# Strassen products in the output stage of a hybrid delta-rule / HGRN2 block

## What is computed

```python
# ya, yb: gated outputs of the two head groups, 512 channels each
y_lat = jnp.concatenate([ya, yb], axis=-1) @ w_out          # 1024 x 1024
x_lat = x_lat + m_lat[2] * y_lat
h_lat = modulate(rms_norm(x_lat, norm2_g), m_lat[3], m_lat[4])
x_lat = x_lat + m_lat[5] * (jnp.square(jax.nn.relu(h_lat @ w_mlp1)) @ w_mlp2)   # 1024 x 4096, 4096 x 1024
return rms_norm(x_lat, final_g)
```

## Time and profile before

| | |
|---|---|
| runs, us | 3981.03, 3980.72, 3990.34 (median 3981.03) |
| span of the profiled execution, first to last instruction | 3976.3 us |
| PE busy | 3551.1 us (89%) |
| DVE busy | 1828.9 us (46%) |
| ACT busy | 1525.4 us (38%) |
| POOL busy | 891.9 us (22%) |
| front stage | 0 to 108 us |
| merge stage | 2282 to 2364 us |
| output stage | 2364 to 3976 us |

### The profile page before, as it was taken

How to read it: one execution, slowest core, us unless ns; L and a number is a source line. 1 busy time by engine, 2 the same in 40 slices (tenths; PEclk the granted TensorE clock), 3 DMA queues, 4 the chain that set the end, 5 groups by cost and what they waited for, 6 DMA issues and landing times. The chain is left out here.

```text
span 3976.3 us, 98790 instructions
## 1 busy us (share of the span) xinstructions
PE 3551.1 (89%) x42320; PEld 2944.9 (74%) x42320; DVE 1828.9 (46%) x2710; ACT 1525.4 (38%) x2048; POOL 891.9 (22%) x872
## 2 busy tenths in 40 slices
PE   6899999999788888857776649999999999999999
PEld 3677888888677777747666238888888888888887
DVE  5488401110055555536555746444544464445443
ACT  5566314332155555513334313333322342234223
POOL 0220233231145545506555102000100100010001
PEclk8899999999899999966778669999999999999999
DMA  6243433452323333333342573434333333333332
GB/s 252 73 81 64 90 109 134 136 138 74 100 90 109 111 103 107 107 100 87 93 99 59 202 243 96 122 96 120 113 117 99 98 112 117 100 96 112 97 99 85
DMA packets 599112, 441.14 MB, mean 111 GB/s; under 512 B 119949, under 2 KB 548305, under 8 KB 591577
## 3 DMA queue, kind: packets, MB, share of 16 engines
q1 hardware_dynamic: 574048, 408.20, 35.3%
q0 software_dynamic: 5632, 16.78, 1.4%
q10 hardware_dynamic: 19192, 12.65, 1.1%
HBM read 338.17 MB, written 99.39 MB: 110 GB/s over the span
## 5 line engine op out<-in xcount | busy, mean ns | idle before, releaser
L618 PE MATMUL p_pg<-h_hi,p_whi 128*128 128x512 f32 (+1 forms) x1384 | 532.1, 384 | 10.0 <-DVE p_wlo L847 10.0
L2639 ACT ACTIVATE o_w_hi<-o_raw 128x1024 fp32r<-128x1024 f32 x288 | 303.6, 1054 | 573.1 <-PE o_pg L2600 558.7
L618 PE MATMUL p_pg<-h_hi,p_wlo 128*128 128x512 f32 (+1 forms) x1384 | 520.2, 376 | 0.0
L618 PE MATMUL p_pg<-h_lo,p_whi 128*128 128x512 f32 (+1 forms) x1384 | 520.1, 376 | 0.0
L2598 PE MATMUL o_pg<-o_f_hi,o_w_hi 128*128 128x512 f32 x1088 | 425.0, 391 | 0.0
L2600 PE MATMUL o_pg<-o_f_hi,o_w_lo 128*128 128x512 f32 x1088 | 423.6, 389 | 0.0
L2599 PE MATMUL o_pg<-o_f_lo,o_w_hi 128*128 128x512 f32 x1088 | 423.5, 389 | 0.0
L2598 PE MATMUL o_pg<-o_h_hi,o_w_hi 128*128 128x512 f32 x1024 | 400.2, 391 | 1.7 <-DVE o_w_lo L2718 1.7
L2600 PE MATMUL o_pg<-o_h_hi,o_w_lo 128*128 128x512 f32 x1024 | 398.7, 389 | 0.0
L2599 PE MATMUL o_pg<-o_h_lo,o_w_hi 128*128 128x512 f32 x1024 | 398.6, 389 | 0.0
L2718 DVE TENSOR_TENSOR o_w_lo<-o_raw,o_w_hi 128x1024 fp32r<-128x1024 f32 x288 | 351.6, 1221 | 58.3 <-ACT o_w_hi L2639 58.3
(11 more groups left out here) (310 smaller groups left out, 6808.0 us busy)
## 6 DMA issues: line engine op xcount, KB each, us to landing
o_raw<-in_w_mlp SPq DMA_DIRECT2D x256, 512.0 KB, 4.1
g_kqvb<-scr_kqv SPq DMA_DIRECT2D x72, 384.0 KB, 3.4
p_raw<-in_w_in SPq DMA_DIRECT2D x38, 512.0 KB, 6.0
g_kqa<-scr_kqv SPq DMA_DIRECT2D x72, 256.0 KB, 3.0
p_mw<-in_w_mod POOLq DMA_DIRECT2D x64, 256.0 KB, 3.3
o_raw<-in_w_out SPq DMA_DIRECT2D x32, 512.0 KB, 4.2
scr_kqv<-p_y SPq DMA_DIRECT2D x24, 576.0 KB, 5.9
scr_hf<-p_y SPq DMA_DIRECT2D x16, 576.0 KB, 5.5
```

The source lines that it names most:

```text
L618: last = nc.tensor.matmul(pg[0:m, bank, 0:n], w[:, q, k, 0:m], h[bank][:, k, :], start=(k == 0 and j == 0), stop=(k == KT - 1 and j == 2))
L2639: nc.scalar.activation(w_hi[:, i % 2], raw[:, i % 2], ACT.Copy).then_inc(w_hi_ready, 1)
```

## The change

The three products of the output stage are computed as 2 x 2 block products by the Winograd form of Strassen's scheme: each operand is cut in four quadrants, seven products of combined quadrants take the place of eight, and the four result quadrants are put together from them.

*Units.* There are 72 units. Each is a 2 x 2 block product with a stationary operand `s` (256 wide: two halves m of 128), a moving operand `t` (1024 wide: two halves n of 512) and a contraction of 1024 (two halves of four pieces of 128). Each unit has seven steps q = 0 to 6, one per product, of 12 matmuls of 128x512 each (hi·hi, hi·lo, lo·hi for four pieces). Units 0 to 7 (M1 = 8) are w_out: s is 256 tokens of y, t the whole weight. Units 8 to 39 are w_mlp1: s is 256 hidden channels of the weight, t the h of 1024 tokens, in two sets of 16 units. Units 40 to 71 are w_mlp2: s is 256 tokens of f, t a quarter of the weight, four sets of 8 units. "x units" are those of w_out and w_mlp2, "f units" those of w_mlp1.

*Operands.* The seven combinations of s are made per unit by POOL (four subtractions or additions of 128x512: `mix_start`, `mix_turn`, `mix_end`) and split per step by ACT (`s_high`) and DVE (`s_low`), one unit ahead. The seven combinations of t (7 x 128x2048) are held for a whole set. At the last unit of a set SP loads the next seven, 1 MB each, one after each step (`t_load`), ACT rounds them (`t_high`, 128x2048), DVE makes five lo parts and POOL two (`t_low`). There are six such **set changes**, at units 7, 23, 39, 47, 55, 63. The combinations of w_mlp2 are made by POOL during the f units (`pre_join`) and kept in device memory (`scr_w2`), those of h by DVE (`join_operands`), kept in `scr_h`; the ones of w_out are made in the merge stage, with the gate of the residual folded in.

*Results.* Products accumulate in four PSUM banks X, Y, V, Z. Step 0 is read out by ACT (`take_p1`), DVE adds banks and partial sums (`combine` at steps 1 to 6). In x units POOL adds three quadrants to x (`x_add`). In f units ACT applies relu and square. x now stands token-major; x1, h and f go through device memory between the units (`scr_x1`, `scr_h`, `scr_f`). In w_out units ACT also squares, scales and reads back the transposed rows (PE `turn`, 16 transposes of 128x128 per unit, after step 4 of the next unit), to make h.

*Elsewhere.* The front stage no longer stores the transposed x (8 stores of 1 MB on SP); semaphores there are allocated in another way. The final norm is applied by DVE to token-major rows; the transposes at the end are gone.

```diff
 def phase_merge(nc, e):
...
+                w_load(0)
+                w_load(1)
+                sp.wait_ge(rows_ready, 1)
+                sp.dma_start(e.sgate[:, :], mrow[:, :]).then_inc(rows_out, 16)
...
+            @block.gpsimd
+            def _(pool):
+                pool.wait_ge(gate_in, 16)
+                done = 0
+                for kk in range(4):
+                    pool.wait_ge(wo_in[kk % 2], 32 * (kk // 2 + 1))
+                    gate = e.o_gate[:, :].rearrange("p (n c) -> p n c", n=2).unsqueeze(2).to_broadcast([P, 2, 2, TB])
+                    nc.gpsimd.tensor_tensor(lo32[:, 0::2, kk, :].rearrange("p (n h) c -> p n h c", n=2),
+                                            wr[:, kk % 2].rearrange("p (n h) c -> p n h c", n=2), gate, ALU.mult).then_inc(wo_gated, 1)
+                    pool.wait_ge(wo_gated, kk + 1)
+                    done = join_operands(pool, lambda q: lo32[:, q, kk, :], wo_joined, done)
...
+                    if b < NB - 1:
+                        act.wait_ge(wo_joined, 4 * b + 4)
+                        nc.scalar.activation(t_hi[:, :, b, :], lo32[:, :, b, :], ACT.Copy).then_inc(wo_hi, 1)
...
 def phase_out(nc, e):
...
+        BANK = (BX, BY, BX, BY, BV, BZ, BV)
...
+        SETS = [0, M1, M1 + N1 // 2] + [M2 + NW * c for c in range(FC)]
+        LAST_OF = {at - 1: k for k, at in enumerate(SETS) if k}
...
+                def t_load(s, q):
+                    sp.wait_ge(product, 7 * (SETS[s] - 1) + q + 1)
...
+                    sp.dma_start(lo32[:, q], src).then_inc(t_in[q], 16)
...
+                        if q == 0:
+                            if i + 2 < N:
+                                raw_load(i + 2)
+                            if 0 <= i - 2 < M1:
+                                h_store(i - 2)
+                            if pre_step(i - 2) is not None:
+                                pre_store(pre_step(i - 2))
+                        if q == 1 and 0 <= i - 1 < N and not final_unit(i - 1):
+                            store(i - 1)
...
+                def multiply(i, q):
+                    pe.wait_ge(s_lo_ready, 7 * i + q + 1)
...
+                    if q == 1:
+                        pe.wait_ge(u3_ready, i)
+                    if q == 2:
+                        pe.wait_ge(p1_ready, i + 1)
+                    if q == 3:
+                        pe.wait_ge(u2_ready, i + 1)
+                    if q == 4:
+                        pe.wait_ge(c12_ready, i)
+                    if q == 5:
+                        pe.wait_ge(c21_ready, i)
+                    if q == 6:
+                        pe.wait_ge(c22_ready, i + 1)
...
+                    for k in range(4):
+                        nc.tensor.matmul(out, s_hi[:, q, k, :], t_hi[:, q, k, :], start=(not more and k == 0), stop=False,
+                                         skip_group_check=more)
+                        nc.tensor.matmul(out, s_hi[:, q, k, :], t_lo[:, q, k, :], start=False, stop=False, skip_group_check=more)
+                        last = nc.tensor.matmul(out, s_lo[:, q, k, :], t_hi[:, q, k, :], start=False, stop=(k == 3),
+                                                skip_group_check=more)
...
+                def scale(i):
+                    act.wait_ge(inv, i + 1)
+                    act.wait_ge(x1_out[i % 2], 16 * (i // 2 + 1))
...
+                        if i + 1 < N:
+                            s_high(i + 1, q)
+                        if i in LAST_OF and q >= 2:
+                            t_high(LAST_OF[i], q - 2)
+                        if i - 1 in LAST_OF and q < 2:
+                            t_high(LAST_OF[i - 1], q + 5)
...
+                        if 0 <= i < N and q:
+                            combine(i, q)
+                        if i + 1 < N:
+                            s_low(i + 1, q)
+                        if i in LAST_OF and q >= 2:
+                            t_low(LAST_OF[i], q - 2)
```

More of the change, by code:

```diff
@@ L2501, in y_of @@
[L2501 to L2510 removed]
+        raw, t_hi, t_lo, gate = e.o_raw, e.o_t_hi, e.o_t_lo, e.o_gate
+        lo32 = e.o_t_raw
+        s_hi, s_lo = sb("s_hi", [P, 7, 4, P], F32R), sb("s_lo", [P, 7, 4, P], F32R)
```

800 lines of the change are left out of this document (453 added, 347 removed).

## The result

| | before | after |
|---|---|---|
| median of 9 runs each, us | 3980.72 (3974.34 to 3990.34) | 3995.45 (3991.71 to 4007.86) |
| profiled span | 3976.3 | 3991.5 |
| PE, DVE, ACT, POOL busy | 3551.1, 1828.9, 1525.4, 891.9 | 3386.4, 2038.0, 1645.9, 1707.9 |
| first product to last product | 2367.52 to 3957.54, 1590.0 | 2398.59 to 3979.16, 1580.6 |

The account below looks back on a forecast made before the run. TensorE's matmuls were taken to bound the output stage; -196 + 19 + 96 + 27 + 33 - 6 = -27 us gave a span of 3949 and a median of 3954 us, 4.7 above the span, range 3890 to 4035.

Parts of the forecast that it names:

- set changes: Six changes of t in the output stage: late loads, rounding and splitting cost 3 x 11 + 3 x 21 = 96 us.
- w_out units: Units 2 to 6: PE waits 5.4 us each before the transposes for x's store behind h's, 27 us in all.
- Products: Output stage: 6048 matmuls instead of 6912 at the old pace of 0.2269 us, 196 us less.
- f units: w_mlp1 units: a lo part waiting for POOL makes ACT's copy 0.6 us late, 31 times, 19 us.
- The chain: f units, steps 4 to 6: DVE combination, ACT relu, square and hi part, DVE lo part, 3.45 us against PE's 2.72.
- Merge stage and filling: Stage ahead of the output stage and its first operands: w_out loads and POOL's work delay the first matmul, +33 us.
- tail: From the last product to the kernel's end: 12.5 us instead of 18.4, so -6 us.
- front: First stage: dropping the x stores could give at most 1.4 us, counted as 0.
- second rival: f units, steps 4 to 6: every lo part waits for POOL at the shared port, 80 us, 4034 us; chance 0.19.
- clock rival: Output stage: after some 11 long waits 12 matmuls run at half speed, 30 us, 3984, no change; chance 0.09.
- port rule: DVE operations with two SBUF inputs and POOL's SBUF reads exclude each other; without it the sum some 35 us lower.
- 3857: Rival that the output stage's waits are mostly covered: terms sum to -124 us, 3895 its likelier form; chance 0.21.

Follow-up runs that it names:

- e4_no_mix: Changed kernel without POOL's four combinations of s, ACT and DVE taking plain quarters instead: 3996.95 us, ratio to before 1.0047.
- e1_x_first: Changed kernel with SP issuing the store of x ahead of the store of h in w_out units: 3957.02 us, ratio to before 0.9946.
- e5_no_w2: Changed kernel without the w_mlp2 work beside the f units (loads, POOL's long product, 1.75 MB stores): 3981.41 us, ratio to before 1.0.
- e10_four: Changed kernel with x stored before h, t split three steps behind its load, merge split one block later, all t low parts on DVE: 3910.61 us.

## Why the prediction was wrong, point by point

The steps that failed are two terms of the sum, the set changes (96 us forecast, 136 measured) and the w_out units (27 forecast, 53 measured). What they had at nothing or too small was DVE's work ahead of a combination that PE needs, with small operations held for 3.6 to 4.4 us by POOL's long ones, and the slow clock behind the waits. These 66 us less the 17.5 that the f units gave back, and some 6 of small terms, took the forecast of -27 to +15.

- **Products**: right, -197 for -196; the pace held.
- **f units**: over-sized, 1.5 for 19. The chain was sized well: ACT's copy of product 0 ends 9.5 and 10.5 us after product 4, unit by unit in turn, for 10.3, and PE has slack in the first and loses 0.09 us in the second. I let one lo part to a unit wait for POOL at steps 5 and 6; the trace shows DVE's means up (1032 and 1141 ns for 0.69), but in places with slack. e4_no_mix shows what it costs when the long operation comes into the narrow place.
- **w_out units**: the wait named, for x's store behind h's, was right in place, and e1_x_first shows it. Its size, 5.8 for 5.4, is partly luck: the forecast had both stores issued at 6 us and only the bytes of h as the hindrance, where SP stood for DVE's additions until 9 us, and PE came to the place 2.5 us later too. What the step left out made it 53 instead of 27: the combination behind DVE's four additions (2.0 a unit), and the fallen clock in the transposes and behind them (about 2.6). The clock stood among the rivals as a case of its own, not as a term. Here it is on the path: with the wait most of that went too, 7.7 a unit in all.
- **Set changes**: under-sized, 136 for 96, all in the same direction. x changes: DVE's combination came at 39.05 for 38, and the time until PE started and its slow step, both left out, made 15 of 11. f changes: the three periods between ACT and DVE were right, 19.8 for 20.5; load 1 was rounded 2.5 us later than put; the rest, small lo part, low part of t and combination, took 8.9 (2988.41 to 2997.27) where I had 3.7 and 2 for the port, since POOL's long product (6.61, part of what e5_no_w2 takes away) held DVE's small one; and the step behind ran slow, 1.7. 28 for 21. Unit 7 and what follows it: 35 for 21. The forecast had only the transposes late there; it left out that DVE makes the four additions of h (9.1 us, one of 4.99 beside POOL's 4.95) ahead of the combination at step 3 of unit 8, where PE waits 11.5. In e10_four, without POOL's low part, that wait is 7.2. e1_x_first took 6 us of the pair and e10_four 14.
- **Merge stage and filling** (+31 for +33), **tail** (-6) and **front** (0; in the two executions profiled the merge stage began at the same time) were right.
- **Rivals.** The port does stretch operations, but in the f units it cost nothing, so the second rival's place was wrong; that the result fell on its side is luck. The clock rival had its size right and too small a chance: 32.8 us of slow matmuls in 23 steps, for the 30 put there, part of it covered.
- **Sums.** Two side figures of the prediction don't add up: without the port rule the terms named come to 19 + 6 x 3 + 3 = 40 us, not 35, and halfway between 3857 and 3954 is 3905, not 3895. The forecast doesn't hang on either.

The Trainium skill, page "SBUF — State Buffer", section "Who interferes with whom", says that a VectorE operation with two SBUF inputs and a GpSimd operation that reads SBUF block each other, the later one until the first is done. The rows agree, 4.28 for 0.69 beside 4.61, and 3.3 for 1.3 on POOL's side. My error at the set changes was not the rule but its size: I charged short waits there, where one short operation behind a long one costs 3.6 to 4.4 us.

The waits, slow steps included, summed to 142 us in the forecast and to 191 in the trace (the rows of the table), and a gain of 196 can't carry waits that are a third larger than counted. What stays open: the share of the loads in a set change, which no run takes away, unit 7 and 8 by all their parts, and why the start of the merge stage varies by 17 us between executions with the same code ahead of it.
